# Modulation units moved from the heads of two layers into the first layer's scan and the gap between the layers

## The reference

```
def modulation(cond, w_ada, b_ada):
    m = jax.nn.silu(cond) @ w_ada + b_ada
    return jnp.split(m[:, None, :], 6, axis=-1)

for i in range(DEPTH):
    sh1, sc1, g1, sh2, sc2, g2 = modulation(cond, w_ada[i], b_ada[i])
    h = rmsnorm(x, norm1_g[i]) * (1 + sc1) + sh1
    y, st = mlstm_mixer(h, ...) if i % 2 == 0 else delta_mixer(h, ...)
    x = x + g1 * y
    h = rmsnorm(x, norm2_g[i]) * (1 + sc2) + sh2
    x = x + g2 * expert_choice_ffn(h, ...)
```

## Time and profile before

| | us |
|---|---|
| median of 3 runs (3250.44 to 3253.73) | 3253.62 |
| span of the profiled execution | 3254.3 |
| PE busy in it | 3039.7 (93%) |
| PE busy with the modulation's matmuls, L760 | 172.0 |
| DVE, ACT, POOL busy | 963.2, 577.3, 96.0 |
| loaded from HBM | 517.89 MB |

### The profile page before, as it was taken

One profiled execution on the slowest core, in us unless ns is written; L12 is line 12 of the kernel. 1 busy time (PEld: TensorE's weight loads), 2 busy tenths in 40 slices (PEclk: granted clock), 3 DMA queues, 4 the chain that ended last, 5 costly groups with the idle time before them and its releaser, 6 DMA issues.

```text
span 3254.3 us, 43264 instructions
## 1 busy us (share of the span) xinstructions
PE 3039.7 (93%) x18405; PEld 2229.6 (69%) x18405; DVE 963.2 (30%) x2408; ACT 577.3 (18%) x1297; POOL 96.0 (3%) x145
## 2 busy tenths in 40 slices
PE   6999999797999999997999989999986999999994
PEld 1465479745887777771456459999944888777773
DVE  1100136643001000102177536666645010001002
ACT  3100111240000000003167212222242000000002
POOL 0000000000000000000000000000000000000000
PEclk9899998897999999998999999999997999999997
DMA  8411100217999999957411100000016899999992
GB/s 281 154 52 52 45 1 1 65 62 270 312 311 303 303 309 308 306 183 271 155 52 52 39 0 1 1 2 1 1 65 224 279 314 304 307 305 307 306 310 87
DMA packets 276365, 545.50 MB, mean 168 GB/s; under 512 B 15233, under 2 KB 23817, under 8 KB 276233
## 3 DMA queue, kind: packets, MB, share of 16 engines
q1 hardware_dynamic: 175049, 328.64, 29.4%
q10 hardware_dynamic: 93600, 188.75, 16.6%
q0 software_dynamic: 7584, 26.22, 3.2%
HBM read 517.89 MB, written 25.70 MB: 167 GB/s over the span
## 4 chain that ended last, share of the span: by engine, by line
PE 88%; DVE 6%; ACT 3%; DMA 2%; issue 1%; SPq 0%; DVEq 0%; POOL 0%; ACTq 0%
PE ps L1204 28%; PE ps L1215 14%; PE ps L803 8%; PE ps L813 6%; PE ps L760 5%; PE ps L1139 3%; PE ps L1101 3%; PE ps L804 2%; PE ps L1083 2%; PE ps L880 1%; PE ps L1115 1%; PE ps L791 1%; PE ps L950 1%; PE ps L966 1%; ACT L424 1%; ACT L423 1%
## 5 line engine op out<-in xcount | busy, mean ns | idle before, releaser
L1204 PEld LDWEIGHTS ps<-wk,slots 128*128 128x128 f32 x6144 | 691.1, 192 | 16.5 <-issue 16.0
L1204 PE MATMUL ps<-wk,slots 128*128 128x80 f32 x6144 | 689.9, 275 | 0.0
L1215 PE MATMUL ps<-qkv,og 128*80 128x512 f32 x1024 | 446.7, 594 | 2.4 <-DVE og L1748 1.3
L1215 PEld LDWEIGHTS ps<-qkv,og 128*80 128x80 f32 x1024 | 151.0, 150 | 275.5 <-issue 268.0
L803 PE MATMUL ps<-hT,slots 128*128 128x512 f32 x640 | 334.0, 604 | 3.1 <-ACT hT L455 3.1
L1204 PE MATMUL ps<-wk,qkv 128*128 128x80 f32 x2048 | 233.9, 275 | 0.0
L1204 PEld LDWEIGHTS ps<-wk,qkv 128*128 128x128 f32 x2048 | 231.3, 192 | 0.0
L804 PEld LDWEIGHTS ps<-hT,slots 128*128 128x128 f32 x640 | 123.5, 193 | 156.6 <-issue 156.6
L813 PE MATMUL ps<-slots,hT 128*128 128x512 f32 x480 | 209.3, 596 | 0.0
L760 PE MATMUL ps<-slots,cnd 128*2 128x512 f32 x384 | 172.0, 602 | 35.1 <-DVE x L1776 24.1
L1724 DVE COPY idc<-idT 80x1 uint32 (+1 forms) x32 | 4.8, 149 | 612.8 <-DMA moe_d<-og,idc 612.7
(11 more groups left out here) (261 smaller groups left out, 3228.5 us busy)
## 6 DMA issues: line engine op xcount, KB each, us to landing
slots<-in_w_gate_dram ACTq DMA_DIRECT2D x60, 2048.0 KB, 9.2
qkv<-in_w_down_dram SPq DMA_DIRECT2D x34, 2048.0 KB, 9.8
slots<-in_w_up_dram SPq DMA_DIRECT2D x32, 2048.0 KB, 10.2
qkv<-in_w_up_dram SPq DMA_DIRECT2D x32, 2048.0 KB, 7.8
qkv<-in_w_down_dram ACTq DMA_DIRECT2D x30, 2048.0 KB, 7.8
slots<-in_w_ada_dram SPq DMA_DIRECT2D x24, 2048.0 KB, 8.1
slots<-in_w_in_dram SPq DMA_DIRECT2D x16, 2048.0 KB, 8.1
slots<-in_w_out_dram SPq DMA_DIRECT2D x4, 2048.0 KB, 16.2
```

The lines of the kernel that those rows point to most:

```text
L1204: ins = mm(PS[:, j, fb * CAP:(fb + 1) * CAP], slot[j][:, kt, fb * P:(fb + 1) * P], xsT[q][:, kt, :], start=(kt == 0), stop=(kt == KT - 1))
L1215: ins = mm(PS[0:CAP, 4 + j, :], hdT[:, ft, :], slot[4 + j][:, ft, :], start=(ft == 0), stop=(ft == KT - 1))
```

## The change

- The two conditions now stand in `cz`, 32 columns wide with 30 zero columns. A unit's eight matmuls write to four groups of 32 PSUM partitions in turn (slices 0 and 4 to the first, 1 and 5 to the second, and so on). ACT copies all 128 partitions, and a matmul with a 0/1 matrix `fold` in place of the transpose adds the four groups' rows and turns them.
- `FIRST` = 4 units of layer 0 are made at the start, `SCAN` = 14 (the other 8 of layer 0 and 6 of layer 1) in steps 0 to 13 of layer 0's scan, and `GAP` = 6 (the rest of layer 1) between the layers. `modT` and `AB` exist once a layer.
- In the scan the units use PSUM bank 1; `exponents` use bank 0 alone and run one step ahead, not two. DVE adds a unit's bias at the end of each step (`ada_md`), for which PE waits before it starts the next unit.
- SP loads the scan's units to slots 0 and 1, and layer 0's `w_out` right behind them.
- ACT issues the loads of `x`, `lmask`, layer 0's `wgt` and `wrt` and six small ones at its start. At a layer's head, ACT's copies of units alternate with its norm tiles.
- In the gap SP issues `wrt` ahead of the units; `wgt` of layer 1 is loaded before the scan.

The plan of the loads and SP's program:

```
+        FIRST, SCAN, GAP = 4, 14, 6
+        PLAN = [[("ada", k) for k in range(FIRST)] + [("in", g) for g in range(NIN)]
+                + [("ada", FIRST + u) for u in range(SCAN)] + [("out", j) for j in range(NOUT)],
+                [("ada", FIRST + SCAN + n) for n in range(GAP)] + [("in", g) for g in range(NIN)] + [("out", j) for j in range(NOUT)]]
...
+                if L == 1:
+                    sp.wait_ge(S("logits"), 1)
+                    sp.dma_start(wrt[:, :, :], a["w_router"][L].rearrange("(k p) e -> p k e", p=P)).then_inc(S("wr_in"), 16)
...
+                    for i in range(FIRST + NIN, len(PLAN[0])):
+                        sp.wait_ge(*slot_free(0, i))
+                        mix_load(0, i)
```

In ACT's program:

```
+            def ada_rows(k, bank):
+
+                act.wait_ge(S("ada_mm"), k + 1)
+                A(mrow[k % 2], PS[:, bank, :], ACT.Copy).then_inc(S("ada_ev"), 1)
...
-                norm(2 * L)
-                modulation(L)
+                if L == 0:
+                    for k in range(FIRST):
+                        ada_rows(k, k % 2)
+                        norm_tile(0, k)
+                    norm_tile(0, NT - 1)
+                else:
+                    for n in range(GAP):
+                        ada_rows(FIRST + SCAN + n, 4 + n % 2)
+                        if n >= 2:
+                            norm_tile(2, n - 2)
+                    norm_tile(2, NT - 1)
```

In PE's program, the unit, the scan's loop and the heads of the layers:

```
-                    for kt in range(KT):
-                        ins = mm(PS[0:2, n % 2, :], cnd[:, 1, kt:16:8], slot[j][:, kt, :],
-                                 start=(kt == 0), stop=(kt == KT - 1))
+                for kt in range(KT):
+                    q = 32 * (kt % 4)
+                    ins = mm(PS[q:q + 32, bank, :], cz[:, kt, :], w[:, kt, :], start=(kt < 4), stop=(kt >= 4))
+                ins.then_inc(S("ada_mm"), 1)
+
+            def ada_cols(k, bank, at):
+
+                pe.wait_ge(S("ada_ev"), k + 1)
+                for b in range(4):
+                    ins = mm(PS[:, bank, at + 2 * b:at + 2 * b + 2], mrow[k % 2][:, b * P:(b + 1) * P], fold[:, :], start=True, stop=True)
+                ins.then_inc(S("ada_tr"), 1)
...
                 for n in range(20):
                     if n + 1 < 20:
                         scores(n + 1)
-                    if n + 2 < 20:
-                        exponents(n + 2)
+                    if n < SCAN:
+                        if n:
+                            pe.wait_ge(S("ada_md"), n)
+                        ada_rows(FIRST + n, 1)
+                    if n + 1 < 20:
+                        exponents(n + 1)
                     back(n)
+                    if n < SCAN:
+                        ada_cols(FIRST + n, 1, 0)
...
+                if L == 0:
+                    pe.wait_ge(S("cond"), 1)
+                    modulation(0, FIRST, 0)
+                    pe.wait_ge(S("setup2"), 16 * 7)
+                else:
+                    pe.wait_ge(S("o_ready"), PER["o_ready"])
+                    modulation(FIRST + SCAN, GAP, 4)
+                    pe.wait_ge(S("x_moe"), NT)
```

In DVE's scan:

```
                     end(n)
+                    if n < SCAN:
+                        dve.wait_ge(S("ada_tr"), FIRST + n + 1)
+                        ada_bias(*ada_unit(FIRST + n), 1, PS[:, 1, 0:8]).then_inc(S("ada_md"), 1)
+                dve.wait_ge(S("ada_md"), SCAN)
+                ada_scale(0, 1)
+                ada_scale(1, 0).then_inc(S("ab"), 1)
```

More of the change, by code:

```diff
@@ L102, in backbone @@
         convT = vecT[:, 144:264].rearrange("p (j c) -> p j c", j=TAPS)
-        cnd = sb("cnd", [P, 3, 16])
-        modT = sb("modT", [P, MOD, 2])
-        AB = sb("AB", [P, 2, KT, 2])
+        cnd = sb("cnd", [P, 16])
+        cz = sb("cz", [P, KT, 32])
+        fold = sb("fold", [P, 2])
+        modT = [sb(f"modT{L}", [P, MOD, 2]) for L in range(2)]
+        AB = [sb(f"AB{L}", [P, 2, KT, 2]) for L in range(2)]
         ss = sb("ss", [P, 4, 16])
@@ L424, in inverse_root @@
                 return A(dst, dst, ACT.Exp, scale=-0.5)
+            act.dma_start(x[:, 0, :], a["x_prompt"][0]).then_inc(S("x_in"), 16)
+            act.dma_start(x[:, 1:5, :], a["x_sample"][0].rearrange("(t p) d -> p t d", p=P)).then_inc(S("x_in"), 16)
+            act.dma_start(lmask[:, :, :], a["lmask"]).then_inc(S("setup2"), 16)
+            act.dma_start(wgt[:, :, :], w_in(0)[:, :, 4 * D:4 * D + 32]).then_inc(S("wg_in"), 16)
+            act.dma_start(wrt[:, :, :], a["w_router"][0].rearrange("(k p) e -> p k e", p=P)).then_inc(S("wr_in"), 16)
+            with nc.allow_non_contiguous_dma(reason="small vectors"):
+                for dst, src in (
+                    (gb0[:, :, 0, :], a["mlstm_ig_b"][0].partition_broadcast(P)),
+                    (gb0[:, :, 1, :], a["mlstm_fg_b"][0].partition_broadcast(P)),
+                    (gb1[:, :, 0, :], a["delta_A_log"][0].partition_broadcast(P)),
+                    (gb1[:, :, 1, :], a["delta_dt_bias"][0].partition_broadcast(P)),
+                    (m0[:, :, :], a["state_mlstm_m"][0, 0].partition_broadcast(P)),
+                    (dng[:, :], a["delta_norm_g"][0].partition_broadcast(P)),
+                ):
+                    act.dma_start(dst, src).then_inc(S("setup2"), 16)
             act.wait_ge(S("vec"), 1)
             act.wait_ge(S("epst"), 1)
-            A(cnd[:, 0, :], vecT[:, 32:48], ACT.Exp, scale=-1.0).then_inc(S("cexp"), 1)
+            A(cnd[:, :], vecT[:, 32:48], ACT.Exp, scale=-1.0).then_inc(S("cexp"), 1)
             def norm(i):
@@ L455, in evac_tile @@
                     A(hT[:, kt, t * P:(t + 1) * P], PS[:, 2 * (t % 2) + 2, kt * P:(kt + 1) * P], ACT.Identity,
-                      scale=AB[:, k, kt, c:c + 1], bias=modT[:, 24 * k + kt, c:c + 1]).then_inc(S("hta"), 1)
+                      scale=AB[L][:, k, kt, c:c + 1], bias=modT[L][:, 24 * k + kt, c:c + 1]).then_inc(S("hta"), 1)
             def proj(L):
@@ L969, in scan_mlstm @@
                 exponents(0)
-                exponents(1)
                 scores(0)
@@ new lines, in ada_scale, with modulation @@
+            def ada_scale(L, k):
+                return V.scalar_tensor_tensor(AB[L][:, k, :, :], modT[L][:, 8 + 24 * k:16 + 24 * k, :], 1.0,
+                                              norm_g[:, k, L, :].unsqueeze(2).broadcast_to([P, KT, 2]), ALU.add, ALU.mult)
+            def modulation(L, first, count):
+                dve.wait_ge(S("ada_tr"), first + count)
+                link(ada_bias(L, first % NADA, count, PS[:, 6, 0:8 * count]))
+                ada_scale(L, L).then_inc(S("ab"), 1)
+                dve.wait_ge(S("ab"), 1 + 2 * L)
@@ L1315, in evac_tile @@
                 dst = hT[:, 4:8, t * P:(t + 1) * P]
-                link(V.tensor_tensor(dst, four(PS[:, 2 * (t % 2) + 3, :]), heads(AB[:, k, 4:8, c]), ALU.mult))
-                V.tensor_tensor(dst, dst, heads(modT[:, 24 * k + 4:24 * k + 8, c]), ALU.add).then_inc(S("htv"), 1)
+                link(V.tensor_tensor(dst, four(PS[:, 2 * (t % 2) + 3, :]), heads(AB[i // 2][:, k, 4:8, c]), ALU.mult))
+                V.tensor_tensor(dst, dst, heads(modT[i // 2][:, 24 * k + 4:24 * k + 8, c]), ALU.add).then_inc(S("htv"), 1)
             def gates_mlstm():
```

200 lines of the change are left out of this document (95 added, 105 removed).

## The result

The changed kernel takes 3184.32 us (median of 4 runs, 3182.96 to 3186.91), the kernel before 3253.68 beside it (3250.44 to 3255.05). The ratio is 0.9783, with a 95% interval of 0.9768 to 0.9798: 69 us or 2.2% faster. That lies in the range from 3165 to 3262; the forecast of 3213 was 29 us too high. The profiled execution has a span of 3181.1 us, with a mean granted clock of 0.949 (before 0.958).

The account below looks back on a forecast made before the run. PE was taken as the bound at layer heads and in the scan, with DMA not the limit. Gains 70.7 + 57.1 + 5.1 minus 29.5 and 16 A gave 40.7 us off 3254.3, forecast 3213, range 3165 to 3262.

Parts of the forecast that it names:

- A: PE time of one unit's 16 passes, put at 3.92 us within bounds of 1.74 and 6.96; this case's chance 0.48.
- the second pass waits for the first, all behind it wait too: In a unit on PE, a pass waiting for its column group blocks later ones, giving 9 × 0.435 = 3.92 us.
- all four groups at once: Rival for the unit's price: column groups run fully side by side, 1.74 us a unit, 3178 us in total; chance 0.28.
- The ring: Scan: PE's unit waits for DVE's previous bias, closing a loop, so a step takes 10.0 + A.
- the slow clock: Scan: steps with a lowered PE clock add 1.04 us a step on average, making the step 11.0 + A.
- no ring: Scan rival: DVE gets ahead, so the wait closes no loop; 1.2 us less in 13 steps, 16 us faster than each case.
- The changes of shape: Scan: 28 switches of PE's array shape cost 0 to 4.8 us, taken as 0.
- The head: Start of layer 0: projection starts at 54.2 + A in place of 124.88, a gain of 70.7 − A.
- ACT first issues eleven DMAs: Layer 0's start: ACT's load issues precede the exponential for `cz`, which ends near 20 us (15 to 24).
- The gap: Between layers: six units instead of twelve, layer 1's projection at 1534.0 + A in place of 1591.07, gain 57.1 − A.
- The tail: Layer 0 after the scan: the 5.7 us wait for `w_out` goes, DVE's scale instructions cost 0.6; gain 5.1 us.
- One after another: Rival: a unit's tiles do not overlap, A = 6.96, time 3265 us, decisive from A = 6.5 on; chance 0.24.

Follow-up runs that it names:

- e1_pairs: Changed kernel with a unit's tiles reordered so that two successive matmuls go to the same column group: 3186.74 us, ratio 0.9785 to the kernel before.
- e10_two: Changed kernel with a unit's eight matmuls sent to two column groups in turn, the fold reading those two: 3211.46 us, ratio 0.9864 to the kernel before.
- e3_noring: Changed kernel where ACT copies the folded unit out of PSUM and PE waits for that copy, not DVE's bias: 3173.04 us, ratio 0.9754 to the kernel before.
- e5_wout_late: Changed kernel with layer 0's w_out loaded behind the scan again instead of during it: 3191.31 us, ratio 0.9794 to the kernel before.
- e2_one: Changed kernel with all eight matmuls of a unit sent to one column group, the fold reading it alone: 3287.17 us, ratio 1.0094 to the kernel before.
- e4_issues: Changed kernel with eight small loads at layer 0's head issued by SP behind the third unit's load, not by ACT: 3189.44 us, ratio 0.9797 to the kernel before.

## Why the prediction was right or wrong

- **What bounds the kernel, and where the units were worth moving: right.** Each gain and the one loss lie in the stage and have the sign that was put, and with A = 1.92 the sum is −72.7 against −73.2. That it comes so close is luck: the head gave 5.8 us less than the sum has, and the projection of layer 0, which it puts at nothing, 4.4 more; the others differ by 0.4 to 2.2 either way.
- **A, 3.92: wrong; it moves the sum by 32 us, the size of the miss.** The step that failed is "the second pass waits for the first, all behind it wait too". From the earlier trace rows, where all passes went to one group, it could not be read whether a waiting pass blocks the others; I chose that it does. e1_pairs shows that it does not, in an order made to provoke it. The rival of all four groups at once (1.74 and 3178) had the mechanism; its sum was 6 us under the measured time. Of the page "TensorE: Matmul & The Clock Gate" (the Trainium skill, Part 3, Packing small matmuls) the rule that tiles run at once agrees: four groups give 7.05 / 1.92 = 3.7 times. Its other sentence, that matmuls start and end in program order, does not agree with e1_pairs, where the second matmul to a group has to start after the first of the next; the measurement decides. A unit that takes 3.6 us gives 3211 (e10_two): the forecast was right for a price that this kernel does not have.
- **The scan: right, for steps at full clock.** The ring was seen, with a wait of about 1 us (1.07) and a step of 10.0 + A, which holds for three values of A. But PE waits so in only four of 13 steps; in eight the low clock makes PE's own work the bound. The mean step was to be 11.0 + A, which with A = 1.92 is 12.9, and is 12.71: the slow clock added 0.88 a step, not 1.04. That the four-group case had 12.7 is chance, since its A was 1.74. Its last rival, no ring, was to be 1.2 us shorter a step; e3_noring, which cuts the ring, is 1.14 shorter at full clock. The changes of shape, put at nothing, are at most the 0.23 us a step that e3_noring has beside the unit and the folds. The weights were no bound, and the folds and ACT's activations cost nothing while DVE was later, as put.
- **The head: 5.8 us short.** `cz` was to come near 20, 24 at the worst, and came at 25.5; this is the term "ACT first issues eleven DMAs": 16.1 us by its working (6.95 + 5.29 + 9 x 0.43), while they lasted from 0.8 to 23.2. `wgt` took 0.58 us and not 6.95, but `wrt` took 6.64, the first of the six small vectors 6.15 and not 0.43, and three others 1.51 to 3.13. The rest of that sum holds: 28.90 for the first copy, then 53.22 − 28.90 = 24.3 against 23.2 + 1.6, then 8.6 against 8.0.
- **The gap: right in sum (−54.8 against −55.2) and in its course.** The last landing came 34 us behind DVE's first row, as put (1514 − 1480.30 = 33.7; now 1494.16 − 1460.01 = 34.2), `wrt` took no time to speak of, and two norm tiles stood behind it. That these two were only a matter of ACT's order, worth 5.4 us, was not seen.
- **The tail: right, but for the clock.** 5.1 was put and the wait went; another 2 us are passes that ran slower behind it, at a granted clock of 0.50 (e5_wout_late).
- **One after another, 3265: its price was wrong too.** It was 22 us too low, because a formula with A once at the head and once in the gap counts on covers that end when a unit is longer than what runs beside it. Between e10_two and e2_one, drawn as a line, the change breaks even near A = 5.6, not 6.5.
- **The projection of layer 0: put at nothing, and 4.4 us shorter.** Of these, 1.1 are the exponents of the second step, which stood ahead of the first scores and now stand behind them; the rest is the clock. Why the low stretch is longer in some traces stays open.

## What to carry to other kernels

Matmuls with two useful columns need not run one after another: eight of them spread over the four groups of 32 PSUM partitions took 1.92 us in place of 7.05, and the four small matmuls that fold them 0.95. When a wait is put into a loop, write down the ring that it closes, with the lengths from one step of the trace; here it gave the step at full clock to 0.1 us for the three prices that were tried. A term that counts a price once because other work covers it needs the price at which the cover ends beside it.

## What was not expected of the hardware

- The order in which the groups are addressed made no difference in the two orders tried: 0 0 1 1 2 2 3 3 took 1.94 us and 0 1 2 3 0 1 2 3 took 1.92.
- The same small load can be slow or quick to issue, on SP and on ACT: `wgt` took 5.29 us on SP in e4_issues and 0.58 on ACT in the changed kernel; there `wrt` and a vector's load took 6.64 and 6.15 on ACT, while `wrt` of layer 1 took 0.43 on SP in the gap. What sets the length was not tested.
- A wait of 5.4 us on PE cost about 2.5 us more behind it: 16.41 against 13.90 for the next 32 passes, the first 4.51 us of them at a granted clock of 0.50.
